# Attention's scores two pairs ahead of their use, its exponentials one, and the value projection behind the dense layer

## The reference

```python
x = x + mlstm_mixer(rmsnorm(x, g0), ...)
x = x + swiglu_dense(rmsnorm(x, g1), ...)
shared = nsa_shared_kv(rmsnorm(x, norm_kv), ...)      # keys, values; compressed keys, values
x = x + nsa_mixer(rmsnorm(x, g2), shared, ...)        # per head: compressed, selected, window
x = x + moe_swiglu(rmsnorm(x, g3), ...)
return rmsnorm(x, norm_final)
...
o_cmp = softmax(q @ k_cmp.T * scale - slope * dist) @ v_cmp
o_slc = softmax(q @ k_slc.T * scale - slope * dist) @ v_slc
o_win = softmax(q @ k_win.T * scale - slope * dist) @ v_win
return g0 * o_cmp + g1 * o_slc + g2 * o_win
```

## Time and profile before

| | us |
|---|---|
| three runs, median (lowest to highest) | 1364.48 (1364.33 to 1365.29) |
| the profiled execution | 1363.06 |
| its span, first to last instruction | 1361.3 |
| busy PE / DVE / ACT / POOL | 1320.7 / 763.7 / 643.4 / 31.3 |

### The profile page before, as it was taken

How to read it: one execution, slowest core, us unless ns; L and a number is a source line. 1 busy time by engine, 2 the same in 40 slices (tenths; PEclk the granted TensorE clock), 3 DMA queues, 4 the chain that set the end, 5 groups by cost and what they waited for, 6 DMA issues and landing times.

```text
span 1361.3 us, 18942 instructions
## 1 busy us (share of the span) xinstructions
PE 1320.7 (97%) x7610; PEld 1002.3 (74%) x7610; DVE 763.7 (56%) x912; ACT 643.4 (47%) x771; POOL 31.3 (2%) x96
## 2 busy tenths in 40 slices
PE   7999999998999988999999999999999999999997
PEld 7987888887987677777776666777666777666762
DVE  6855645544647557973367635367645357654332
ACT  5646544434456546662356533356534255644221
POOL 5000000001000000000000000000000000000000
PEclk9999999999999898999999999999999999999999
DMA  8543555555452127899999999999999999999996
GB/s 355 171 170 105 204 186 186 185 185 185 156 217 80 45 85 264 332 363 429 427 427 427 424 414 426 428 426 428 428 417 425 427 427 428 427 418 424 428 428 275
DMA packets 36086, 431.67 MB, mean 317 GB/s; under 512 B 4000, under 2 KB 4000, under 8 KB 5152
## 3 DMA queue, kind: packets, MB, share of 16 engines
q1 hardware_dynamic: 35856, 429.94, 78.3%
q10 hardware_dynamic: 144, 0.52, 0.1%
HBM read 429.40 MB, written 1.05 MB: 316 GB/s over the span
## 4 chain that ended last, share of the span: by engine, by line
PE 90%; DVE 4%; ACT 2%; DMA 2%; issue 1%; POOL 0%; POOLq 0%; SPq 0%; DVEq 0%; ACTq 0%
PE bank L1602 20%; PE bank L1604 19%; PE bank L1603 19%; PE bank L2171 13%; PE bank L2192 7%; PE bank L1988 1%; DMA raw<-in_moe 1%; PE bank L2121 1%; PE bank L2218 1%; PE bank L1972 1%; DVE w_lo L1507 1%; PE bank L1928 1%; PE bank L2229 1%; DVE ht_lo L1027 1%; PE bank L1890 1%
## 5 line engine op out<-in xcount | busy, mean ns | idle before, releaser
L1507 DVE TENSOR_TENSOR w_lo<-raw,w_hi 128x2048 fp32r<-128x2048 f32 x114 | 257.9, 2287 | 151.2 <-ACT w_hi L902 150.9
L1602 PE MATMUL bank<-w_hi,ht_hi 128*128 128x512 f32 (+1 forms) x768 | 304.3, 396 | 3.3 <-DVE ht_lo L1305 1.1
L1604 PE MATMUL bank<-w_hi,ht_lo 128*128 128x512 f32 (+1 forms) x768 | 296.6, 386 | 0.0
L902 ACT ACTIVATE w_hi<-raw 128x2048 fp32r<-128x2048 f32 x114 | 214.3, 1909 | 135.2 <-DMA raw<-in_moe 120.5
L1003 DVE TENSOR_TENSOR w_lo<-raw,w_hi 128x2048 fp32r<-128x2048 f32 x70 | 159.6, 2288 | 112.3 <-ACT w_hi L592 112.3
L1603 PE MATMUL bank<-w_lo,ht_hi 128*128 128x512 f32 (+1 forms) x568 | 218.2, 384 | 0.0
L1602 PEld LDWEIGHTS bank<-w_hi,ht_hi 128*128 128x128 f32 x768 | 144.5, 188 | 48.0 <-issue 17.8
L592 ACT ACTIVATE w_hi<-raw 128x2048 fp32r<-128x2048 f32 x71 | 135.5, 1918 | 90.8 <-PE bank L1604 88.9
L1604 PEld LDWEIGHTS bank<-w_hi,ht_lo 128*128 128x128 f32 x768 | 144.4, 188 | 30.1
L1507 DVE TENSOR_TENSOR more_lo<-more,w_hi 128x2048 fp32r<-128x2048 f32 x50 | 114.1, 2289 | 80.6 <-ACT w_hi L902 80.5
L902 ACT ACTIVATE w_hi<-more 128x2048 fp32r<-128x2048 f32 x50 | 95.9, 1918 | 101.4 <-DMA more<-in_moe 54.3
(11 more groups left out here) (325 smaller groups left out, 1510.3 us busy)
## 6 DMA issues: line engine op xcount, KB each, us to landing
raw<-in_moe SPq DMA_DIRECT2D x112, 2048.0 KB, 13.1
more<-in_moe SPq DMA_DIRECT2D x54, 2048.0 KB, 12.9
raw<-in_wts SPq DMA_DIRECT2D x71, 1024.0 KB, 4.8
more<-in_moe SPq DMA_DIRECT2D x4, 1024.0 KB, 14.7
xs<-in_x SPq DMA_DIRECT2D x2, 512.0 KB, 3.9
out<-xn SPq DMA_DIRECT2D x4, 256.0 KB, 2.0
pk<-in_packed SPq DMA_DIRECT2D x1, 517.0 KB, 7.6
g1b<-in_norm_ffn ACTq DMA_DIRECT2D x1, 512.0 KB, 3.5
```

The costliest lines, as they stand in the source:

```text
L902: a(w_hi[:, hi_order(n) % SPLIT, :], slot_raw(n), ACT.Copy).then_inc(s_hi, 1)
L1507: v.tensor_tensor(slot_lo(n), slot_raw(n), w_hi[:, hi_order(n) % SPLIT, :].bitcast(F32), ALU.subtract).then_inc(s_lo, 1)
L1602: mm(out_, sh, mh, start=first, stop=False)
L1604: return mm(out_, sl, mh, start=False, stop=last)
```

## The change

1. The values' two slots move from 65 and 66 to 53 and 54, right behind the dense layer's; keys are then 55 to 58, queries 59, 60, 65, 66, compression 61 to 64. `EXTRA_FREE` names KV0+4 instead of VV0+2.
2. The last two slots of the dense layer are used together, tile by tile (`down_two`), and residual, square, norm, transposes and gains go by tile (`stream_turned`, `stream_high`, `stream_low`). The values' products stand between the tiles' transposes and before the keys.
3. In attention, PE's scores stand two pairs ahead (`pair_banks` alternates throughout), ACT's exponentials one pair ahead of the copies. In PE's list products of the pair before stand ahead of the transposes. No values are left there.
4. All pair products go to bank 6. The output projection of tile 0 has both halves in bank 7 (`OUT_BANKS`), so its second half waits for DVE's residual of the first, which is moved into the loop's last pass.
5. Splits of BO0 and BO0+1 stand ahead of attention; those of the other two one pass earlier. ACT's copies of the compressed values (`vbd`) stand behind the first two heads' exponentials, and `cmp_scores` waits for the keys' copies alone.

```diff
-    FF0, DN0, KV0, W10, VV0, BO0, N0 = 20, 42, 53, 59, 65, 67, 71
-    Q_SLOT = (57, 58, 63, 64)
+    FF0, DN0, VV0, KV0, W10, BO0, N0 = 20, 42, 53, 55, 61, 67, 71
+    Q_SLOT = (59, 60, 65, 66)
...
-    EXTRA_FREE = (VV0 + 2, VV0 + 2, N0, N0 + 1)
+    EXTRA_FREE = (KV0 + 4, KV0 + 4, N0, N0 + 1)
...   DVE, dense layer to keys
+        residual(1, (0, 1, 2, 3), VV0 - 1, (0, 1))
+        normed_tile(2, 0)
+        stream_low(3, 0, (0, 1))
+        residual(1, (0, 1, 2, 3), VV0 - 1, (2, 3))
+        stream_low(3, 0, (2, 3))
+        normed_tile(2, 1)
...   PE, dense layer to keys
-        transposed(3, 6)
+        down_two(DN0 + 9, (0, 1, 2, 3), 18, False, True, {(1, 1, 0): lambda: stream_turned(0)}, None, ath, atl)
+        values(0, 0)
+        stream_turned(1)
+        values(1, 0)
+        values(0, 1)
+        values(1, 1)
+        pe.wait_ge(s_htl, turned_count(4, 0, 3))
...   ACT, attention
+        head_exp(0)
+        head_exp(1)
+        for r in range(R):
+            a(vbd[...]...)
         for p in range(2 * HP):
-            head_exp(2 * p)
-            if p:
-                turned_copied(2 * p - 1)
+            if p + 1 < 2 * HP:
+                head_exp(2 * p + 2)
+            if p in (0, 5):
+                cmp_exp(p // 5)
+            turned_copied(2 * p + (p < HP))
+            if p + 1 < 2 * HP:
+                head_exp(2 * p + 3)
+            if p >= HP:
+                turned_copied(2 * p + 1)
...   DVE, attention
         for p in range(2 * HP):
+            if p == 10:
+                final_low(0)
+                final_low(1)
+            if p == 2 * HP - 1:
+                residual(2, OUT_BANKS, N0 - 1, (0,))
...   PE, attention
-        values(0, 0, range(KD))
-        pe.wait_ge(s_kc, 6)
+        pe.wait_ge(s_kc, 2)
         cmp_scores(0)
         for p in range(HP):
+            pair_scores(p + 2)
             if p:
-                pair_scores(p + 1)
+                pair_products(p - 1)
             probs_turned(2 * p + 1)
             if p == 0:
-                values(1, 0, range(KD))
                 cmp_transposed(0)
-            if p >= 2:
-                for i, k in late_values[...]:
-                    values(i, 1, (k,))
...
         for p in range(HP, 2 * HP):
-            if p + 1 < 2 * HP:
-                pair_scores(p + 1)
-            probs_turned(2 * p)
+            if p + 2 < 2 * HP:
+                pair_scores(p + 2)
             if p >= 11:
                 first_tile_out((2 * p - 22,))
             pair_products(p - 1)
             if p >= 11:
                 first_tile_out((2 * p - 21,))
+            probs_turned(2 * p)
             probs_turned(2 * p + 1)
```

More of the change, by code:

```diff
@@ L350, in pair_banks @@
     def pair_banks(p):
-        return (B[0], B[1]) if p < HP and p % 2 else (B[2], B[3])
-    def pairs_before(p):
-        return p - 2 if p < HP else HP - 2 if p == HP else p - 1
+        return (B[0], B[1]) if p % 2 else (B[2], B[3])
     def turn_bank(item):
@@ L387, in num_banks, with turned_at, turned_count, shared @@
         return (B[4], B[5]) if h == HA - 1 else (B[6], B[7])
+    def turned_at(t, k):
+        if t == 0:
+            return B[4 + k // 2][:, (k % 2) * P:(k % 2 + 1) * P]
+        return B[2 + k // 4][:, (k % 4) * P:(k % 4 + 1) * P]
+    def turned_count(p, t, b):
+        return 24 + TURNED.index((p, t, b)) + 1
+    def shared(t, b):
+        return b if t == 0 else b | 1
     def tile_ready(engine, sem_, c, t, n):
@@ L728, in _, with stream_high @@
         dense_high(5)
[L729 to L733, removed]
+        split_to(VV0 + 1)
+        def stream_high(p, t, pairs):
+            for b in pairs:
+                if p == 3:
+                    act.wait_ge(s_xt, 20 + 4 * t + shared(t, b) + 1)
+                else:
+                    act.wait_ge(s_htl, turned_count(3, t, shared(t, b)))
+                for k in (2 * b, 2 * b + 1):
+                    ins = a((hk_hi if p == 3 else ht_hi)[:, k, t * P:(t + 1) * P], turned_at(t, k), ACT.Copy,
+                            scale=pk[:, C_GAIN + 8 * p + k:C_GAIN + 8 * p + k + 1])
+                ins.then_inc(s_hth, 1)
+        square(2, 0, 4)
+        stream_high(3, 0, range(4))
+        stream_high(4, 0, (0, 1))
+        square(2, 1, 4)
+        split_to(KV0)
+        stream_high(3, 1, range(4))
+        stream_high(4, 0, (2, 3))
+        stream_high(4, 1, range(4))
+        split_to(KV0 + 1)
+        for t in range(NT):
+            act.wait_ge(s_used, VV0 + 2)
+            a(vv[:, t, :, :], B[t][:, :].rearrange("p (b d) -> p b d", b=2), ACT.Copy).then_inc(s_vvc, 1)
         for i in range(4):
@@ L756, in _ @@
         act.wait_ge(s_used, W10 + 4)
-        a(hid[:], B[6][:, 0:CH], ACT.Silu).then_inc(s_hid, 1)
+        a(hid[:], B[3][:, 0:CH], ACT.Silu).then_inc(s_hid, 1)
         act.wait_ge(s_sf, 1)
@@ L771, in _ @@
               ACT.Copy).then_inc(s_kc, 1)
[L772 to L782, removed]
+        split_to(BO0)
         def cmp_exp(t):
@@ L1184, in _, with stream_low @@
         dense_low(5)
[L1185 to L1190, removed]
+        split_to(VV0 + 1)
+        def stream_low(p, t, pairs):
+            hi, lo = (hk_hi, hk_lo) if p == 3 else (ht_hi, ht_lo)
+            for b in pairs:
+                dve.wait_ge(s_hth, turned_count(p, t, shared(t, b)))
+                for k in (2 * b, 2 * b + 1):
+                    ins = v.scalar_tensor_tensor(lo[:, k, t * P:(t + 1) * P], turned_at(t, k),
+                                                 pk[:, C_GAIN + 8 * p + k:C_GAIN + 8 * p + k + 1],
+                                                 hi[:, k, t * P:(t + 1) * P].bitcast(F32), ALU.mult, ALU.subtract)
+                ins.then_inc(s_htl, 1)
+        residual(1, (0, 1, 2, 3), VV0 - 1, (0, 1))
[4 more added lines that the diff above has]
+        normed_tile(2, 1)
+        stream_low(4, 0, (0, 1))
+        stream_low(3, 1, range(4))
+        split_to(KV0)
+        stream_low(4, 0, (2, 3))
+        stream_low(4, 1, range(4))
+        split_to(KV0 + 1)
         def token_blocks():
@@ L1288, in pair_out @@
             t, h = head(2 * p)
-            bank = out_bank(p)
+            bank = B[6]
             if p:
@@ L1689, in down, with down_two @@
             ins.then_inc(s_used, 1)
-        def down_two(n, banks, kt0, first, last, turns, fresh=None):
+        def down_two(n, banks, kt0, first, last, turns, fresh=None, hi=hth, lo=htl):
             for t in range(NT):
@@ L1977, in pair_products @@
             t, h = head(2 * p)
-            g, first, bank = h // R, h % R, out_bank(p)
-            pe.wait_ge(s_vvc, t + 1)
+            g, first, bank = h // R, h % R, B[6]
+            pe.wait_ge(s_vvc, 2)
+            pe.wait_ge(s_kc, 6)
             if p:
-                pe.wait_ge(s_ev, p if p <= HP else p - 1)
+                pe.wait_ge(s_ev, p)
             pe.wait_ge(s_atc, max(copied_turns(prob_turn(2 * p + 1)), copied_turns(("c", t))))
```

142 lines of the change are left out of this document (65 added, 77 removed).

## The result

| | before | after |
|---|---|---|
| median (lowest to highest), us | 1364.4 (1362.4 to 1365.3), 4 runs | 1385.26 (1380.71 to 1388.08), 4 runs |
| the profiled execution, us | 1363.06 | 1380.71 |
| its span, us; mean granted clock | 1361.3; 0.991 | 1379.0; 0.979 |

The ratio is 1.0156, 95% interval 1.0137 to 1.0174: the change makes the kernel slower by 21 us. The forecast was 1368.5, the range 1357.5 to 1377: right in sign, too small in size, and the measured time lies above the range. The profiled execution is the shortest of the four; the others had mean clocks of 0.974 and 0.975, and where they lost the rest no trace shows.

A forecast was written before the change was run, and what follows sets the result against it. The prediction took the expert transfer stream, started when PE frees the output projection's slots, as the bound. A held-clock sum of -7.0 plus 10.5 cold surcharge gave +3.5, taken as +4 on 1364.5: 1368.5 us, range 1357.5 to 1377.

The forecast's parts named there:

- The bound: Expert transfers, started when PE frees the output projection's slots: time won or lost before 501 us moves the end one for one.
- Dense layer to keys: Between last dense matmul and keys: 14.7 us instead of 5.86, clock held (-1.7), so all behind comes 7.2 us later.
- Attention's start: Before the compressed probabilities' transposes: PE stands 3.5 us without the values as cover; 9 in 10 that the clock falls.
- The cold stretch: Attention's tile 0 at low clock, 4.5 us per pair, back before products of pair 5: 10.5 us surcharge; chance 0.40.
- warm sum: Whole change if the clock holds: attention -14.2 us, stage before +7.2, together -7.0.
- late: Rival: clock low until the output projection's matmuls or late in tile 1; +8 to +21, 1372.5 to 1385.5 us; chance 0.19.
- The tail behind pair 10 is PE's work in the old order: End of attention, behind pair 10: no change, taken as 0.
- clock holds: Rival: clock stays up in attention or is back within two pairs; -7.0, or -6 to -3; 1357.5 to 1361.5 us; chance 0.24.
- The pair of 2.4 us: Attention's tile 0 where the clock holds: bank 6 sets 2.4 us per pair, PE's own work 2.2.
- pair 8 to 9: Tile 1 of attention, with two transposes of `xo`: 5.6 us between starts of products where the clock holds.
- That wait goes: PE's 2.41 us wait before 449.27 disappears, as an early split leaves DVE's list ahead of it.
- -7.0 + 10.5 = +3.5: Whole change: sum with the clock held plus cold surcharge; with part of the next pair taken as +4.

The follow-up runs named there:

- e3_both: Changed kernel with 28 unused matmuls in PE's 3.43 us idle gap and ACT's splits of the last two output slots one pass earlier: 1363.35 us.
- e1_fill: Changed kernel with 28 matmuls of 256 columns, results unused, in PE's 3.43 us idle gap at attention's start: 1369.55 us.
- e2_splits: Changed kernel with ACT's splits of the output projection's last two slots one pass earlier, DVE's left in place: 1379.25 us.
- e12_late: e2_splits with 28 filling matmuls of 256 columns behind the idle gap, at pair 1's transposes: 1370.34 us.
- e10_turned1: e9_turned with one head's transposes ahead of the products of the pair before in tile 1 too: 1356.56 us.
- e6_banks: e5_order with products of tile 0's odd pairs in bank 7 instead of bank 6: 1364.27 us.
- e11_old_split: Kernel before the change, with the second output slot's split one pass earlier in DVE's and ACT's lists: 1361.0 us.
- e13_old_low: e11_old_split with DVE's two subtractions for the turned outputs ahead of pair 11's bias: 1355.36 us.
- e8_fill14: e3_both with 14 filling matmuls instead of 28: 1375.7 us.
- e4_turns: Changed kernel with 30 transposes of a constant, no matmuls, in PE's idle gap at attention's start: 1369.38 us.
- e9_turned: e6_banks with tile 0's PE order as next scores, transposes, then products of the pair before: 1362.87 us.
- e5_order: e3_both with PE's next scores behind the products of the pair before in tile 0: 1366.44 us.

## Why the prediction was right or wrong

- **The bound** (stream of experts, started by PE's output products): right but for 1.5 us. Transfers of the earlier trace rows moved by 16.2 us, the span by 17.7; in e3_both they came 1.8 earlier and the end 0.3.
- **Dense layer to keys**: right. The dense place ends at about 331.8 (332.63 less the 0.87 of eight transposes), keys start 14.5 later; 14.7 was predicted, with clock 1.00. That all comes 7.2 later shows in e3_both, +7.3 at the first scores; in the execution of after it was +5.1, as its dense layer had ended 2.0 earlier.
- **Attention's start**: right, 3.43 us against 3.5, and so was that the clock falls there. e1_fill shows what this wait cost: 15.7 us.
- **The cold stretch**: the mechanism right, its size wrong. A pair took 4.8 us instead of 4.5, scores of 512 columns did not bring the clock back at pair 5, and it fell again at 457. From pair 0 to pair 10, 54.2 us instead of the forecast's 47.2: +7.0. Of this 3.2 is the warm sum's (below); against e3_both's 40.6 the cold clock cost 13.6, where I had 9.8. The clock came back with the scores of 512 columns, as forecast, but one pair later, before pair 6; in e2_splits it came back only at pair 8's products, in tile 1, as the rival "late" had it. So the pair at which it comes back was no sound term: which of the two a run takes, no trace explains. e12_late shows that dense matmuls bring it back sooner. Why it fell again at 457, behind a wait of 0.74 us only, stays open; in e3_both it held behind the same wait.
- **"The tail behind pair 10 is PE's work in the old order", taken at no change, is the step that failed**: from pair 10 to pair 15 it cost 8.1 us. It is not the old order: both heads' transposes now stand behind the products, so their copies, which end ACT's pass, come late, and ACT's split with them, while DVE's list reaches the same split early. I had counted splits "one pass earlier" as a gain on DVE's list only. e2_splits, which moves ACT's alone, took out the wait of 2.54 us and the stretch behind it and won 6 us; the other 1.6 stay in e3_both (29.2 us against before's 27.65). e10_turned1, with the order restored as well, made the tail 1.6 us shorter than before's.
- **The warm sum, -7.0**: wrong too, so that the rival "clock holds" would have missed: e3_both gave -1.0 (span -0.3). By the same marks: start +0.4, pairs 0 to 10 +3.2 (40.6 us for 37.4), tail +1.6, from there to the end +1.5. The pair of 2.4 us came from bank 6, with PE's own work put at 2.2 beneath it; 2.2 holds in the old order only, where compressed matmuls and scores lie side by side. In the new one PE itself needs 2.86, 0.46 more in each of the two plain pairs at the start. The largest single miss is pair 8 to 9, 6.8 us for 5.6, with two waits for ACT's copy; pair 3 to 4 was 1.1 shorter than I had it. The wait of 1.56 us at bank 6, before pair 5's products (the expectation of e6_banks has it as pair 6's), was not in the sum as such; pair 4 to 5 took 4.7 us for 4.1. e10_turned1 came to -7.6, near my -7.0, but with other orders and other terms (pairs 0 to 10 38.6 us, tail -1.6), so it does not bear out the sum.
- **"That wait goes"** (2.41 us before pair 9's products): it went, but I had given half of the reason. The early split alone does not remove it (e11_old_split); it needs the subtractions ahead of the bias too (e13_old_low), which the change has and I had not priced.

The sums meet: from the -7.0 + 10.5 = +3.5 of the forecast, less 2.1 for where the profiled execution stood at attention's start, plus 6.6 up to pair 10, plus 8.1 and 1.5 behind it, comes 17.6; 17.7 was measured. These are spans of one execution; the median of after lies 4.6 us above it, and no trace shows that part.

## What to carry to other kernels

Before taking dense matmuls out of a stage of transposes and narrow products, find the longest wait that they cover: here 3.4 us uncovered cost 15.7 us, and 3.6 us of useless matmuls in its place won them back, as they end when the awaited probabilities are there. When one engine's list is reordered, walk the lists of the others for a job done by two of them (a split in ACT and DVE): if one reaches it early and the other late, everything behind it on the early one waits. And look first for the small waits: two moves in the old kernel's lists won what the whole rewrite won after it was mended.

## What the hardware showed that was not expected

- With PE busy 24.00 of 24.00 us, the granted clock stayed at 0.50, the level of 1.2 GHz, while the work was transposes, products of 64 columns and scores. With such work it came back after 34 us in after, after some 50 in e2_splits, and within 4 in e8_fill14; 28 matmuls of 256 columns brought 1.00 back within 4.6 us (e12_late).
- Transposes in the gap held the clock as matmuls did: 1369.38 (e4_turns) against 1369.55 (e1_fill). The Trainium skill, "TensorE: Matmul & The Clock Gate", Part 4, says that transposes do not count as busy time for the gate in the way that matmuls do; here, for holding the clock over this gap, the measurement shows no difference.
- A wait of 1.77 us left the outcome open: mean clock 0.990 and 0.992 in two executions, 0.979 to 0.983 in six, 6.5 to 14.8 us apart (e8_fill14). Shorter waits went either way as well: 1.10 us (held in e3_both, a fall behind it in e9_turned) and 0.74 (held in e3_both, a fall in after).
- Two matmul groups on 64 rows each, from different operands, ran side by side when adjacent: starts 0.01 us apart, 0.85 us for both, against 1.26 in a row. In e5_order that won nothing, as ACT's copy then lay open.
